# Interleaving FFN1's normalization and transposes with the first block's gate/up matmuls, per token group

## The reference

```
h = x
h = h + 0.5 * swiglu_1(rms_norm(h))          # FFN1: gate and up 1024 -> 2816, down 2816 -> 1024
u = rms_norm(h) @ w_in                       # q 512 | k 128 | v 128 | pooled channels 512
h = h + concat(window_attention(q, k, v), multiscale_pool(u)) @ w_out
h = h + 0.5 * swiglu_2(rms_norm(h))          # FFN2, the same sizes
out = rms_norm_final(h)
swiglu(x) = (silu(x @ w_gate) * (x @ w_up)) @ w_down
```

## Time and profile before

| what | value |
|---|---|
| runs | median 2744.25 us of 3 (2703.81, 2744.25, 2820.25) |
| profiled execution | 2704.3 us, span of its slowest core 2702.2 us |
| spans of the 8 cores | 2684.0 to 2702.2 us |
| mean granted PE clock of the cores | 0.962 to 0.966 |
| PE busy | 2387.7 us, 88% of the span |
| DVE busy | 1018.4 us, 38% |
| ACT busy | 780.6 us, 29% |
| POOL busy | 207.8 us, 8% |
| chain that ended last | PE 75%, ACT 6%, issue 6%, DMA 6%, DVE 5% |

### The profile page before, as it was taken

The page is one execution under the profiler, slowest core; times in us unless marked ns, Lnnn a source line. Parts: engine busy times, 40 slices in busy tenths (PEclk is TensorE's granted clock), DMA queues, the critical chain, the costliest instruction groups (busy, mean ns, idle before and its releaser), DMA issues.

```text
span 2702.2 us, 33524 instructions; the slowest of 8 cores (2684.0 to 2702.2 us)
## 1 busy us (share of the span) xinstructions
PE 2387.7 (88%) x11845; PEld 1103.3 (41%) x12076; DVE 1018.4 (38%) x1635; ACT 780.6 (29%) x1536; POOL 207.8 (8%) x250
## 2 busy tenths in 40 slices
PE   4999888899769998899967998889995999888997
PEld 2444434344334444444433444434442444443443
DVE  3323356233323335623342333652234223552333
ACT  3111267210421017611152102761115111662103
POOL 0000000000300000000030000000003000000003
PEclk9999989999979999999988999999997999998999
DMA  5556300443554330044455433004444554004433
GB/s 133 84 89 101 64 1 1 70 71 60 113 127 75 66 59 1 1 70 71 77 126 110 70 59 59 1 1 73 83 79 132 98 86 74 1 1 70 71 60 89
DMA packets 61282, 181.00 MB, mean 67 GB/s; under 512 B 5056, under 2 KB 5184, under 8 KB 61120
## 3 DMA queue, kind: packets, MB, share of 16 engines
q0 software_dynamic: 51040, 144.23, 31.7%
q1 hardware_dynamic: 10080, 34.62, 4.0%
HBM read 306.27 MB, written 16.78 MB: 120 GB/s over the span
## 4 chain that ended last, share of the span: by engine, by line
PE 75%; ACT 6%; issue 6%; DMA 6%; DVE 5%; POOL 1%; SPq 0%; DVEq 0%; ACTq 0%; POOLq 0%
PE ps L293 22%; PE ps L297 22%; PE ps L323 20%; PE ps L562 5%; DMA out<-H 3%; PE ps L397 2%; DVE JUNK L350 2%; PE pst L378 2%; DMA H<-x 1%; ACT HID L474 1%; ACT RDEN L498 1%; DVE HID L304 1%; DMA WGU<-wgu 1%; DVE XNT L382 1%; DVE MIXT L509 1%
## 5 line engine op out<-in xcount | busy, mean ns | idle before, releaser
L293 PE MATMUL ps<-XNT,WGU 128*128 128x512 bf16 (+1 forms) x2923 | 673.6, 371 | 11.3 <-DMA WGU<-wgu 4.2
L297 PE MATMUL ps<-XNT,WGU 128*128 128x512 bf16 (+2 forms) x2946 | 668.3, 368 | 2.7 <-issue 0.4
L323 PE MATMUL ps<-WD,HID 128*128 128x512 bf16 x2753 | 623.1, 380 | 53.2 <-DVE HID L304 31.0
L302 ACT ACTIVATE SG<-ps 128x512 bf16<-128x512 f32 x374 | 213.9, 572 | 1488.1 <-PE ps L293 1485.1
L304 DVE TENSOR_TENSOR HID<-ps,SG 128x512 bf16<-128x512 f32 x374 | 246.9, 660 | 988.2 <-PE ps L297 960.3
L327 DVE SCALAR_TENSOR_TENSOR H<-ps,H 128x512 f32<-128x512 f32 x512 | 353.9, 691 | 298.4 <-PE ps L323 294.4
L323 PEld LDWEIGHTS ps<-WD,HID 128*128 128x128 bf16 x2816 | 263.2, 97 | 410.3 <-issue 159.2
L293 PEld LDWEIGHTS ps<-XNT,WGU 128*128 128x128 bf16 x2992 | 288.3, 99 | 339.1 <-issue 21.6
L297 PEld LDWEIGHTS ps<-XNT,WGU 128*128 128x128 bf16 x2992 | 287.2, 98 | 327.7 <-issue 8.0
L71 POOL DMA_DIRECT2D WGU<-wgu x176 | 93.8, 534 | 1904.5 <-PE ps L297 1891.9
L378 PE MATMUL pst<-IDB,XN 128*128 128x128 bf16 x768 | 73.2, 252 | 162.5 <-DVE XNT L382 103.0
(11 more groups left out here) (75 smaller groups left out, 986.6 us busy)
## 6 DMA issues: line engine op xcount, KB each, us to landing
WGU<-wgu POOLq DMA_DIRECT2D x176, 512.0 KB, 5.6
WD<-wd POOLq DMA_DIRECT2D x16, 1536.0 KB, 12.9
WD<-wd POOLq DMA_DIRECT2D x16, 1280.0 KB, 10.1
H<-x SPq DMA_DIRECT2D x32, 512.0 KB, 4.7
out<-H SPq DMA_DIRECT2D x32, 512.0 KB, 5.1
WIN<-win POOLq DMA_DIRECT2D x1, 2560.0 KB, 31.2
WOUT<-wout POOLq DMA_DIRECT2D x1, 2048.0 KB, 24.4
BPOOL<-bpool POOLq DMA_DIRECT2D x1, 640.0 KB, 16.0
```

What stands on the lines that cost most here:

```text
L293: tg = P.op("pe", lambda e, k=k, bg=bg, o=o, nn=nn, wv=wv: e.matmul(out=PS[bg][:, 0:nn], lhsT=wv[:, 0, k, :], rhs=XNT[:, k, o:o + nn], sta ...
L297: tu = P.op("pe", lambda e, k=k, bu=bu, o=o, nn=nn, wv=wv: e.matmul(out=PS[bu][:, 0:nn], lhsT=wv[:, 1, k, :], rhs=XNT[:, k, o:o + nn], sta ...
L302: ts = P.op("act", lambda e, bg=bg, nn=nn, ss=ss: e.activation(out=SG[:, ss, 0:nn], in_=PS[bg][:, 0:nn], func=AF.Silu), waits=[tg, sg_free ...
L323: td = P.op("pe", lambda e, ci=ci, bd=bd, li=li, nh=nh, nb=nb: e.matmul(out=PS[bd][:], lhsT=HID[:, ci, li * 128:(li + 1) * 128], rhs=WD[:, ...
```

## The change

`ffn` gets a `group_hook`. With it, in the first block, the first 4 chunks are worked off group by group: for each token group the hook plans the `Nt` of that group's tiles, with the `Na` of tile li+4 behind each, and then come the pairs of chunks 0 to 3 on that group. Only after all groups of the four chunks are their four slots' reloads planned, and behind these the `WD` transfer. Chunks 4 and 5 and all other blocks go chunk by chunk as before. The body of a pair is moved into `plan_group` without change. In pass 0 `late_sp` is planned after FFN1 instead of before it. FFN2 passes no hook.

```diff
-        def ffn(n, tiles, xnt_toks, on_last_tile=None):
+        def ffn(n, tiles, xnt_toks, on_last_tile=None, group_hook=None):
...
+            def plan_group(slot, tok_gu, ci, o, nn):
...
+                w0 = [tok_gu, xnt_toks[lastli]] + bank_free[bg] + bank_free[bu]
...
+                return tu, th_
...
+                if b == 0 and group_hook is not None:
+                    nbatch = 4
+                    last_tu = {}
+                    for gi, (o, nn) in enumerate(groups):
+                        group_hook(gi)
+                        for ci in range(nbatch):
+                            g = g_base + ci
+                            tu, th = plan_group(g % 4, gu_tok[g], ci, o, nn)
+                            last_tu[ci] = tu
+                            last_gate_up = tu
+                    for ci in range(nbatch):
+                        g = g_base + ci
+                        gu_done[g] = last_tu[ci]
+                        plan_gu_load(g + 4)
+                    tok_wd = plan_wd()
+                    rest_ci = list(range(nbatch, nb))
+                else:
+                    rest_ci = list(range(nb))
...
-                    if b == 0 and ci == 1:
+                    if b == 0 and ci == 1 and tok_wd is None:
                         tok_wd = plan_wd()
...
-            for li, t in enumerate(a_tiles):
-                xt.append(Nt(na[t], 0, XNT[:, :, li * 128:(li + 1) * 128]))
-                if li + 4 < len(a_tiles):
-                    t4_ = a_tiles[li + 4]
-                    na[t4_] = Na(t4_, RING_A, xn_free, sq_eng=("dve" if t4_ % 2 == 0 else "act"))
+            def hook(gi, a_tiles=a_tiles, na=na, xt=xt):
+                for li in range(gi * 4, min(gi * 4 + 4, len(a_tiles))):
+                    t = a_tiles[li]
+                    xt.append(Nt(na[t], 0, XNT[:, :, li * 128:(li + 1) * 128]))
+                    if li + 4 < len(a_tiles):
+                        t4_ = a_tiles[li + 4]
+                        na[t4_] = Na(t4_, RING_A, xn_free, sq_eng=("dve" if t4_ % 2 == 0 else "act"))
+            xnt_free = ffn(0, a_tiles, xt, group_hook=hook)
             if p == 0:
                 late_sp()
-            xnt_free = ffn(0, a_tiles, xt)
```

More of the change, by code:

```diff
@@ L263, in ffn @@
             last_gate_up = None
+            def plan_group(slot, tok_gu, ci, o, nn):
+                wv = WGU[:, slot, :].rearrange("p (g k j) -> p g k j", g=2, k=8)
+                pr = state["pair"] % 2
+                state["pair"] += 1
+                bg, bu = 2 * pr, 2 * pr + 1
+                lastli = (o + nn) // 128 - 1
+                w0 = [tok_gu, xnt_toks[lastli]] + bank_free[bg] + bank_free[bu]
+                tg = tu = None
+                for k in range(8):
+                    tg = P.op("pe", lambda e, k=k: e.matmul(
+                        out=PS[bg][:, 0:nn], lhsT=wv[:, 0, k, :], rhs=XNT[:, k, o:o + nn],
+                        start=(k == 0), stop=(k == 7)), waits=w0 if k == 0 else (), inc=(k == 7))
+                for k in range(8):
+                    tu = P.op("pe", lambda e, k=k: e.matmul(
+                        out=PS[bu][:, 0:nn], lhsT=wv[:, 1, k, :], rhs=XNT[:, k, o:o + nn],
+                        start=(k == 0), stop=(k == 7)), inc=(k == 7))
+                ss = state["sgs"] % 2
+                state["sgs"] += 1
+                ts = P.op("act", lambda e: e.activation(
+                    out=SG[:, ss, 0:nn], in_=PS[bg][:, 0:nn], func=AF.Silu), waits=[tg, sg_free[ss]])
+                th_ = P.op("dve", lambda e: e.tensor_tensor(
+                    out=HID[:, ci, o:o + nn], in0=PS[bu][:, 0:nn], in1=SG[:, ss, 0:nn], op=ALU.mult),
+                    waits=[tu, ts])
+                bank_free[bg] = [ts]
+                bank_free[bu] = [th_]
+                sg_free[ss] = th_
+                return tu, th_
             for b, chunks in enumerate(BLOCKS):
@@ L276, in ffn @@
                 th = None
+                g_base = state["gu"]
+                state["gu"] += nb
                 for ci, c in enumerate(chunks):
[L278 to L283, removed]
+                    assert gu_seq[g_base + ci] == (n, c)
+                if b == 0 and group_hook is not None:
[16 more added lines that the diff above has]
+                    rest_ci = list(range(nb))
@@ L284, in ffn @@
+                for ci in rest_ci:
+                    g = g_base + ci
                     tu = None
                     for (o, nn) in groups:
[L286 to L309, removed]
+                        tu, th = plan_group(g % 4, gu_tok[g], ci, o, nn)
                     gu_done[g] = tu
```

## The result

The changed kernel took 2737.63 us (median of 9 runs, 2729.74 to 2752.2), the kernel before 2705.17 (median of 10 runs). The ratio is 1.0125, with a 95% interval of 1.0101 to 1.0149. In some executions of most kernels here, the one before included, cores ran at a lower granted clock and took tens to hundreds of microseconds longer; the ratios leave these out, so a ratio can be small beside a large median. The forecast was 2717, a ratio of 1.005: the time is in the range of 2694 to 2757, but the move was forecast as 13.3 us. The profiled execution has a span of 2738.9 us on its slowest core, against 2702.2, which is 36.7 more.

The account below looks back on a forecast made before the run. PE was 88% busy, idling before transposes at a 2.49 us cycle per tile ahead of FFN1's matmuls. Passes 0 to 3 add 4.6 + 1.9 + 2.8 + 4.0 = +13.3 to 2704.3: 2717 us, range 2694 to 2757.

Parts of the forecast that it names:

- Group 0's start: First gate matmuls of FFN1 start at 36.2, 756.5, 1423.35 and 2087.3 us, 47.2 us sooner in all.
- Batched transposes stay exposed: Tiles 4 to 7 are transposed in a row behind group 0, at 2.49 us a tile, 10.0 us for four.
- Rival 3: Late tiles' transposes are hidden, PE pays 1.01 us for each of 16: 2673 us in all; chance 0.04.
- The clock falls in the batch: PE's clock falls during the second batch of transposes; the restart behind it costs 1.5 us.
- rival 1: PE's clock holds through transposes and stalls, so restarts cost nothing and transposes are quicker: about 2702 us; chance 0.22.
- The third pair's wait in passes 1 and 2: Pair 2 waits for pair 0's product, its SiLU behind tile 7's `XN` on ACT: 3.6 us in pass 1.
- Chunk 4's weights in pass 0: Chunk 0's slot comes free at 80.5, a load takes 5.1, so chunk 4 starts at 85.8, narrow pairs ending at 84.0.
- `WD` behind four loads: Before the first down matmul, `WD` queued at 2.8 us per 512 KB lands about with chunk 5's end, without further cost.
- Rival 2: `WD` becomes the bound, reloads and `WD` landing without overlap: +39, 2756 us with the rest; chance 0.13.
- `late_sp`, the moved body, the table loads in pass 0: The later `late_sp`, the pair's moved body and pass 0's two added ACT table loads of 1.28 us cost nothing.

Follow-up runs that it names:

- e4: Changed kernel with `WD` early, late tiles' transposes between gate and up matmuls, last normalizations behind the first pair, later groups chunk by chunk: ratio 0.9866 to the kernel before.
- the fillers: 6 extra matmuls of 512 columns, result unused, behind each tile's transposes in the second and third batch, added to e1: ratio 1.0037 to the kernel before.
- e6: e1 with the groups behind group 0 worked off chunk by chunk, so that chunk 0's slot comes free sooner in pass 0: ratio 1.0039 to the kernel before.
- e1: Changed kernel with `WD` issued behind the first pair of chunk 0, ahead of the four reloads: ratio 1.0083 to the kernel before, median 2721.27 us.
- e8: e4 with the normalizations of tiles 5 and 6 planned behind tile 3's transposes instead of among them: ratio 0.9861 to the kernel before.

## Why the prediction was right and wrong, step by step

- **Group 0's start.** Right: 35.78 for 36.2; in pass 1 it came 22.1 us behind the pass's first transposes, where the forecast had 23.9.
- **Batched transposes stay exposed.** Right, though 51.47 to 61.42, 9.95 us for 9.96, agrees that well by chance: the row at 61.42 lacks its first matmul, and the batch took some 9.5. In passes 1 to 3 it took 9.1, 9.5 (a row of 7 again, so 9.1) and 6.6 us, for 10.0, 10.0 and 7.5. In every pass its first tiles still ran at high clock (0.61 us instead of 1.01). Rival 3 falls; of the orders tried, only transposes placed between matmuls are hidden (e4).
- **The clock falls in the batch.** Right, and rival 1 falls: the windows at 0.50. Group 1's first pair took 2.5, 1.6 and 2.5 us more than 3.46 in passes 0 to 2, and 1.5 more than 2.6 in pass 3, for 1.5 each. The Trainium skill, page TensorE: Matmul & The Clock Gate, section Part 4: PE-mode transpose, has transposes not counting as busy in the same way. The trace agrees with it, but since the fillers also took away the idle time, no run here tells the two reasons apart.
- **The third pair's wait in passes 1 and 2.** Right: 4.14 and 5.13 us for 3.6 and 4.1. ACT in pass 1 of the changed kernel, with the first SiLU right behind tile 7's copy as forecast:

```profile
772.46 1.15 ACT L390 ACTIVATE XN<-H,ST 128x1024 bf16<-128x1024 f32 x1
773.63 1.28 ACT L283 ACT_TABLE_LOAD   x1
774.92 1.09 ACT L283 ACTIVATE SG<-ps 128x512 bf16<-128x512 f32 x2
```

- **Chunk 4's weights in pass 0.** Right in kind, too small: a wait of 1.8 us was forecast, 5.55 measured. (The row at 89.44 lacks its first matmul, so the wait was some 5.1.) The narrow pairs took 0.89 us each (80.16 to 82.83 for three) and not 1.17, which is the price of a narrow pair with a wide one behind it, the load took 6.9 and not 5.1, and a cold restart behind the wait (7 matmuls in 3.19 us again) was left out. e6 shows the whole of it: 8 us.
- **`WD` behind four loads: the step that failed.** The prediction had `WD` tie with the last product in each pass, "no further cost, and no slack". It did not: PE waited 2.63, 4.93, 5.23 and 8.29 us for `WD` behind its last gate/up matmul, 21.1 in all, where before it waited 3.7 for the product. The term that was mis-sized is the time from the issue of chunk 3's reload to the landing of `WD`, 13.5 us (5.1 for the reload, 2.8 for each 512 KB of `WD`), taken from a single pair of rows. In passes 1 to 3 it was 17.9, 18.2 and 19.3 us: the reload, with others ahead of it in the queue, took 7.0, 8.0 and 8.7, and `WD` 3.4 to 3.6 for each 512 KB. In pass 0, from the first reload's issue, 28.3 us went by (81.76 to 110.05) where 21.9 were forecast. These four come to 21.3 us, nearly the 22 by which the sum is short. The DMA issues of the changed kernel in passes 0 (its first reload, and `WD`) and 2 (`WD`, and chunk 3's reload; KB each, us from issue to landing):

```profile
WGU<-wgu POOLq DMA_DIRECT2D x1, 512.0 KB, 6.9
...
WD<-wd POOLq DMA_DIRECT2D x1, 1536.0 KB, 25.1
```

```profile
WD<-wd POOLq DMA_DIRECT2D x1, 1536.0 KB, 17.7
WGU<-wgu POOLq DMA_DIRECT2D x1, 512.0 KB, 8.0
```

The kernel before could have told this. On the same core, in pass 0, `WD` landed 17.6 us after its issue at 66.31, which is 10.9 behind the reload ahead of it, or 3.6 for each 512 KB:

```profile
WD<-wd POOLq DMA_DIRECT2D x1, 1536.0 KB, 17.6
```

On all cores it took 15.0 to 17.9 us there. In pass 1 it took 15.7, 17.6, 15.0 and 15.6 on cores 0, 1, 3 and 6, and 13.0 to 13.4 on the others; core 4, the one profiled in the page, had the quickest. With 3.6 us per queued 512 KB in place of 2.8, and 6.9 for pass 0's first load, an estimate by the prediction's own working is some 27 us instead of 13.3 (0.8 more for each of six queued steps in pass 0 and of three in each other pass, and 1.8); with the longer reloads of passes 1 to 3 (1.9, 2.9 and 3.6 more) it is 35.5.
- **Rival 2**, `WD` as the bound, was thus the case that came, at a little over half its price: 22 us on top of the forecast's sum, of 39. It had 0.13. The forecast's tie without slack in all four passes should have given it the larger chance: where four estimates all end in a tie, the error of the term goes to one side only.
- **`late_sp`, the moved body, the table loads in pass 0**: no sign of a cost from these, as forecast. Of the two table loads one ran beside pass 0's second batch and one beside group 1's first pair (54.84 and 64.70), and PE waited for neither. Tile 8's sum of squares did cost some 0.4 us: it stands on DVE ahead of tile 5's eviction, and the next transposes waited 1.90 us where others waited 1.48.

Open: why a queued 512 KB took 2.8 us in one place and 3.4 to 3.6 in others. In the kernel before, four of the five cores that issued pass 1's `WD` between 785.1 and 787.6 us were slow (15.0 to 17.6), and the three that issued it at 775.4 to 778.2 were quick (13.1 to 13.4); but core 4, the last of the five, was quick too. Each core's times count from its own first instruction, and no run varied the cores' distance, so contention among cores is argued and not shown.

## What to carry to other kernels

When pairs of work are regrouped so that several weight slots are in use together, they come free together, and the transfers queued behind their reloads come late, as `WD` did here; a transfer whose buffer has long been free should be issued ahead of them. Splitting the serial chain of transposes into batches hid nothing here; it was hidden where each link stood among independent matmuls. A sum that ends in ties should take the price of the tied transfer from all passes and cores, not from the row at hand, and count a possible restart of the clock behind waits like those of 2.6 to 5.9 us here.

## What the runs showed of the hardware beyond the forecast

- The granted clock fell within a batch of transposes in which PE was busy for 1.07 of 3 us, with no gap over 1.90 us before the fall; with 6 matmuls in each gap it stayed at 1.00.
- Waits of about the same length did and did not bring the clock down: behind 2.63 and 2.92 us (e1) the 8 matmuls took 3.43 and 3.46 us, behind 2.85 and 3.08 (e8) 1.89.
- A tile's 8 transposes between gate and up matmuls cost PE 0.44 us at full clock (0.86 at the low one), and PE was not idle between them and the up matmuls (e4).
- A `WD` transfer of 1536 KB issued half a microsecond behind four queued reloads of 512 KB landed after 25.1 us; behind reloads spread 3.45 us apart, after 16.6 to 17.7.
